# First attention of a two-block network: scores from stacked fp32r halves, tiles in another order, modulation spread over later stages

## The chip, the cores and the metric

The kernel runs on one core of a Trainium2 chip. The metric is the device time of one execution in microseconds (us), the median of several runs.

## The reference

One sequence of 512 tokens, 1024 wide, passes through three mixers and a lookup of experts. All is float32.

```python
def first_block(x, c, ...):
    for i in range(2):
        h, gate = adaln_norm(x, c, norm_g[i], ada_w[i], ada_b[i])
        y = nsa_mixer(h, ...) if i == 0 else dilated_mixer(h, ...)
        x = x + gate * y
    return rms_norm(x, final_g)
# adaln_norm: shift, scale, gate = split(silu(c) @ w_ada + b_ada, 3)
#             h = rms_norm(x, g) * (1 + scale) + shift
# nsa_mixer: compressed, selected and window attention, 16 query heads, 2 key heads of 64
#            (at 512 tokens the selected and the window branch see every earlier token)
# dilated_mixer: 16 heads, three dilation patterns, groups joined by their softmax sums
def second_block(x, c, ...):
    mod = silu(c) @ ada_w + ada_b            # six parts of 1024
    # sliding-window attention and a short convolution, then:
    h2 = modulate(rmsnorm(x, norm2_g), shift2, scale2)
    x = x + gate2 * peer(h2, ...)            # 8 heads x 16 of 16384 experts per token
```

The three modulation products, `silu(c) @ ada_w`, have 96 blocks of 128 outputs in all: twelve chunks of eight blocks, each chunk the sum of eight weight pieces.

## The kernel before

Weights come as one stream of pieces of 128 x 1024 floats (`stream()`, line 73) into a ring of four buffers, loaded by SyncE in stream order (`ask_pieces`, L211). A buffer is free again when its piece was split (most pieces) or used (raw ones). A split piece becomes two fp32r tiles, its rounded upper half by ScalarE (`split_hi`, L232) and the rest by GpSimd (`split_lo`, L240); a projection is then three fp32r products per 128 x 128 block (L264, L276). Three split pieces can be held, and the list of pieces is fixed, so a stage's engines work in a written order; stages are blocks with a barrier of all engines between them.

The modulation pieces ("ada") are raw. VectorE multiplies each by its column of silu(c) and adds it to a running row sum (`ada_piece`, L322 and L325); TensorE then reduces a chunk over the partitions with 16 one-column f32 instructions (`ada_chunk`, L333). Chunks 0 to 2 belong to the first two stages, the other nine (3 to 11) lie in the first attention as its fillers.

**Stage 2** (L801 on) makes the first mixer's projections, rotates queries and keys into `qr` (ten rows: two of keys, eight of query pairs), does the compressed branch, and ends with the eight `z` units. GpSimd's last work there is the split of the last `z` piece; ScalarE ends it with the last evacuation (L913).

**First attention** (`attention("nsa", ...)`, L1062 to L1275). A unit is one head of one query tile of 128 tokens in one branch (selected or window): 2 branches x 4 tiles x 16 heads = 128 units, in that order, tile i with i+1 key blocks. Two heads share 128 partitions (64 rows each), so the keys are copied first into `ks_pad`, where the other head's rows are zero (L1160, L1179 and the memsets L1206, L1207); the first product waits for these. Of unit n, in the written order of TensorE:

```python
pe.matmul(ps[:, n % SB, 0:len(vb) * P], q, k, start=True, stop=True)   # L1132, f32, 128 x (i+1)*128
# transposes of unit n-3 (L1140), fillers, products with v of unit n-5 (L1152)
```

VectorE takes the masked minimum of the negated scores (L1189), every fourth copy of transposed probabilities (L1112), the modulation filler (`ada_dve`: 0, 0.5, 0.75 or 1 piece per unit with 1, 2, 3, 4 key blocks), and at the end of every eight units the gated result (L1238). ScalarE takes the exponentials with their sum (L1169) and the other copies (L1110), GpSimd the additions into the result (L1248). Scores have three buffers, so TensorE is at most three units ahead.

Later stages: output projection with modulation of `mod[:, 24:96]`, dilated projections (32 units) and attention, output projection, the second block's projections (18 units), window attention, output projection, and the query projection of the lookup (16 units and 16 score groups).

**Last stage** (L2080 on). 128 tiles of the table `u`, then 128 of `v`, each 128 x 1024 floats. SyncE loads tile m into one of three `t_raw` buffers when tile m-3 is lowered; ScalarE makes the upper half (`upper`, L2194), GpSimd the lower (`lower`, L2268), TensorE multiplies: 24 products of 384 columns per `u` tile (L2124), 18 of 512 per `v` tile (`down`, L2160). In the second half, per four tiles, VectorE also weighs (L2430) and lowers (L2436) the weights and adds four gathered rows (L2447), and GpSimd issues four indirect loads of rows (L2289).

Of the kernel before, what the change touches and what calls it, by code (L numbers as in the profile page):

```python
# [28 lines left out]
P = 128  # L29
# [42 lines left out]

def stream():
# [17 lines left out]
    load("ada", 72)  # L91
    load("nsa_out", 8)
    for name, count in (("dq", 8), ("dk", 8), ("dv", 8), ("dz", 8), ("dil_out", 8), ("q2", 4), ("k2", 1), ("v2", 1), ("cc", 4), ("cu", 4), ("cb", 4), ("out2", 8),
                        ("wq", 16), ("subkeys", 2)):
        load(name, count)
# [13 lines left out]
def build(nc, w_stream, consts_in, small_dram, x_in, pos_in, perm_in, u_in, v_in, u_rows, out, gates_dram, gelu_dram):  # L109
    ctx = ExitStack()  # L110
    with ctx:
# [200 lines left out]
        def ada_piece(dve, j, sums):  # L312
# [5 lines left out]
            total = sums[:, chunk % 2, :]  # L318
# [9 lines left out]
        def ada_chunk(pe, chunk, sums, bank):  # L328

            pe.wait_ge(ada_used, (chunk + 1) * KD)  # L330
            for b in range(KD):
                col = chunk * KD + b
                mm = pe.matmul(ps[:, bank, col:col + 1], sums[:, chunk % 2, b * P:(b + 1) * P],  # L333
                               C("ones")[:, 0:1], start=True, stop=True)
# [465 lines left out]

        with phase() as block:  # L801
# [100 lines left out]
            def _(act):  # L902
# [40 lines left out]
                for u in range(15, 23):  # L943
# [9 lines left out]
                    elif u == 20:  # L953
                        cmp_copy(3)
                        for r in Z_RAW:
# [4 lines left out]
            def _(pool):  # L960
# [4 lines left out]
                for u, n in enumerate(parted, 2):  # L965
# [3 lines left out]
                    if 5 <= u < 12:  # L969
                        rope_nsa[1](pool, u - 5)  # L970

# [90 lines left out]
        def attention(tag, block, units, work, finish, finish_pool=None, pe_filler=None, dve_filler=None, ask=0,  # L1062
                      pads=(), pad_units=1, prob_at=WR_AT,
                      act_filler=None, pool_filler=None, pe_first=None, act_first=None, dve_first=None, sink_neg=None):
# [54 lines left out]
            def _(pe):  # L1119
                if pe_first:  # L1120
                    pe_first(pe)
                for n in range(N + LP):
                    if n < N:
# [8 lines left out]
                        pe.matmul(ps[:, n % SB, 0:len(vb) * P], q, k, start=True, stop=True).then_inc(s_done.sem, 1)  # L1132
# [83 lines left out]
        ks_pad = place("ks_pad", WR_AT + 4 * T, [2, 2, T])  # L1216
        nsa_units = []
        for branch, (ku, vt) in enumerate(((0, vs), (1, vw))):
            for i in range(TT):
                for h in range(NH):  # L1220
                    g = h // 8
                    nsa_units.append((qr[:, 2 + h % 8, tile_tokens(i)], ks_pad[:, g, ku, 0:(i + 1) * P],
                                      C("causal")[:, T - (i + 1) * P:T],
                                      [vt[:, b, g * DH:(g + 1) * DH] for b in range(i + 1)], BIG))
# [4 lines left out]
        def nsa_finish(dve, g, o, den, nmax, o_read):  # L1229
            branch, i, half = g // 8, (g // 2) % 4, g % 2  # L1230
# [10 lines left out]
        def nsa_finish_pool(pool, o_read):  # L1241
            for g in range(16):
                i, half = (g // 2) % 4, g % 2
                o_read.wait(pool, g + 1)
                if g >= 8:
                    pool.wait_ge(added, g - 7)
                dst = ot[:, i, half * 512:(half + 1) * 512]
                pool.tensor_tensor(dst, dst, gtmp[:, g % 2, :], ALU.add).then_inc(added, 1)  # L1248

# [1411 lines left out]
```

## Time and profile before

| | us |
|---|---|
| median of 3 runs | 2348.06 |
| lowest, highest | 2342.16, 2350.55 |
| the profiled execution | 2357.37 |
| its span, first to last instruction | 2355.6 |
| TensorE busy in it | 2238.0 |
| VectorE, ScalarE, GpSimd busy | 1530.1, 914.9, 1307.7 |
| first attention, from its first to its last instruction | 219.7 to 446.9 |
| tiles of `v`, first to last product | 1805.7 to 2346.1 |

Positions are microseconds from the start of the profiled span. The span holds all instructions; the profiled execution's own time is 1.8 us longer and 9.3 us above the median of the runs, which had no profile. "Granted clock" is the share of full speed at which TensorE was clocked, 1.00 for 2.4 GHz and 0.50 for 1.2 GHz. In the groups of instructions, `x` is their number, followed by their busy time and the mean duration of one; an f32 product appears as two instructions, an fp32r product as one.

### The profile page before, as it was taken

Reading aid. Unit: us, or ns where it says so; the run is one execution under the profiler, and the core shown is the slowest. Engines: PE = TensorE matmul, PEld = TensorE weight load, DVE = VectorE, ACT = ScalarE, POOL = GpSimd, SP = SyncE. Lnnn points to the kernel's source line nnn. Section 1 sums busy time; section 2 is a strip of 40 time slices with the busy share of each in tenths; the row PEclk is TensorE's granted clock in tenths of the full one; section 3 lists DMA queues with packets and bytes.
Section 4 is the critical chain, followed back from the end, with each engine's and each line's share of the span. In section 5 each row is a group of like instructions: output and inputs, shape, how many; then the busy total and the mean of one; then the engine's idle time right before and its main releaser. Section 6 shows DMA issues by size and latency. Waiting matters only on the chain.

```text
span 2355.6 us, 31939 instructions
## 1 busy us (share of the span) xinstructions
PE 2238.0 (95%) x11801; PEld 1963.8 (83%) x11801; DVE 1530.1 (65%) x2977; ACT 914.9 (39%) x1513; POOL 1307.7 (56%) x691
## 2 busy tenths in 40 slices
PE   4999999889989989889999999999999999999999
PEld 4888787778878878777899999999999778787877
DVE  6625878556215534542399999999993766676656
ACT  2224555332236332532234333455553333333332
POOL 0532010137540234123268888766656999999996
PEclk9999999789999989999999999999999999999999
DMA  7243646323210122022258888899988999999996
GB/s 266 90 138 104 204 157 211 100 75 107 91 62 5 68 72 81 10 81 94 68 176 293 281 278 279 302 362 355 327 329 324 334 347 336 343 343 347 336 340 246
DMA packets 164474, 492.39 MB, mean 209 GB/s; under 512 B 15072, under 2 KB 64608, under 8 KB 162912
## 3 DMA queue, kind: packets, MB, share of 16 engines
q1 hardware_dynamic: 107872, 305.79, 38.1%
q0 software_dynamic: 36864, 134.23, 15.7%
q10 hardware_dynamic: 19584, 50.34, 5.6%
q8 instruction: 94, 1.54, 0.3%
q14 instruction: 60, 0.49, 0.1%
HBM read 437.87 MB, written 52.43 MB: 208 GB/s over the span
## 4 chain that ended last, share of the span: by engine, by line
POOL 19%; PE 16%; DVE 12%; DMA 2%; issue 1%; ACT 0%; DVEq 0%; ACTq 0%; POOLq 0%
POOL t_split L2268 12%; PE ps L2124 10%; POOL arena L2289 7%; PE ps L2142 4%; PE ps L2160 2%; DMA t_raw<-v_table 2%; DVE arena L2355 1%; DVE arena L2346 1%; DVE arena L2347 1%; DVE arena L2386 1%; DVE arena L2351 1%; DVE arena L2342 1%; DVE rope L2324 1%; DVE arena L2381 1%; DVE norm_rows L2324 1%
## 5 line engine op out<-in xcount | busy, mean ns | idle before, releaser
L2268 POOL TENSOR_TENSOR t_split<-t_raw,t_split 128x1024 fp32r<-128x1024 f32 x256 | 628.1, 2454 | 145.2 <-ACT t_split L2194 141.8
L240 POOL TENSOR_TENSOR w_split<-ring,w_split 128x1024 fp32r<-128x1024 f32 x113 | 272.5, 2415 | 510.7 <-ACT w_split L232 499.4
L2124 PE MATMUL ps<-h_hi,t_split 128*128 128x384 f32 x2048 | 537.1, 338 | 5.7 <-ACT e_gel L2200 3.0
L2160 PE MATMUL ps<-t_split,w_split 128*128 128x512 f32 x2304 | 532.6, 391 | 9.7 <-POOL t_split L2268 7.8
L2160 PEld LDWEIGHTS ps<-t_split,w_split 128*128 128x128 f32 x2304 | 429.3, 188 | 112.9 <-POOL t_split L2268 19.6
L264 PE MATMUL ps<-h_hi,w_split 128*128 128x512 f32 x1440 | 451.7, 392 | 0.0
L2194 ACT ACTIVATE t_split<-t_raw 128x1024 fp32r<-128x1024 f32 x256 | 270.3, 1057 | 360.3 <-DMA t_raw<-v_table 230.0
L2124 PEld LDWEIGHTS ps<-h_hi,t_split 128*128 128x128 f32 x2048 | 373.3, 189 | 8.1 <-POOL t_split L2268 4.6
L2124 PE MATMUL ps<-h_lo,t_split 128*128 128x384 f32 x1024 | 343.6, 336 | 0.0
L264 PEld LDWEIGHTS ps<-h_hi,w_split 128*128 128x128 f32 x1440 | 270.4, 188 | 56.5 <-issue 0.7
L264 PE MATMUL ps<-h_lo,w_split 128*128 128x512 f32 x720 | 280.2, 389 | 0.0
L232 ACT ACTIVATE w_split<-ring 128x1024 fp32r<-128x1024 f32 x113 | 119.0, 1057 | 360.0 <-PE ps L264 220.9
L2430 DVE TENSOR_TENSOR arena<-arena 128x1536 f32<-128x1536 f32 x32 | 108.5, 3389 | 168.5 <-DMA arena<-gates_scratch 168.4
L2289 POOL DMA_INDIRECT arena<-v_table,arena x128 | 193.6, 1512 | 20.7 <-issue 20.0
L2124 PEld LDWEIGHTS ps<-h_lo,t_split 128*128 128x128 f32 x1024 | 193.7, 189 | 0.0
L2200 ACT ACTIVATE e_gel<-ps 128x384 f32<-128x384 f32 x128 | 63.0, 492 | 326.6 <-PE ps L2124 294.6
L2447 DVE SCALAR_TENSOR_TENSOR ps<-arena,ps 128x1024 f32<-128x1024 f32 x127 | 163.0, 1283 | 15.1 <-DMA arena<-v_table,arena 8.6
L264 PEld LDWEIGHTS ps<-h_lo,w_split 128*128 128x128 f32 x720 | 135.2, 188 | 28.4 <-issue 0.7
L1152 PE MATMUL ps<-arena 128*128 128x64 f32 x916 | 138.0, 280 | 0.0
L1248 POOL TENSOR_TENSOR arena<-arena,gtmp 128x512 f32<-128x512 f32 x16 | 20.3, 1271 | 205.7 <-DVE gtmp L1238 205.7
L1152 PEld LDWEIGHTS ps<-arena 128*128 128x128 f32 x916 | 132.4, 209 | 2.1
L2421 DVE TENSOR_SCALAR arena<-ps,arena 128x128 f32<-128x128 f32 x384 | 130.5, 401 | 0.0
(317 smaller groups left out, 3199.3 us busy)
## 6 DMA issues: line engine op xcount, KB each, us to landing
ring<-w_stream SPq DMA_DIRECT2D x219, 512.0 KB, 3.4
t_raw<-u_table SPq DMA_DIRECT2D x128, 512.0 KB, 4.6
t_raw<-v_table SPq DMA_DIRECT2D x128, 512.0 KB, 4.9
gelu_scratch<-e_gel ACTq DMA_DIRECT2D x128, 192.0 KB, 4.8
gates_scratch<-arena ACTq DMA_DIRECT2D x8, 3072.0 KB, 12.7
arena<-gelu_scratch SPq DMA_DIRECT2D x32, 768.0 KB, 5.4
arena<-gates_scratch SPq DMA_DIRECT2D x32, 768.0 KB, 8.8
xT<-x_in SPq DMA_DIRECT2D x2, 1024.0 KB, 10.8
```

The source lines that it names most:

```text
L232: act.activation(w_split[:, i % RS, 0, :], ring[:, n % R, :], ACT.Copy).then_inc(hi_done, 1)
L240: pool.tensor_tensor(w_split[:, i % RS, 1, :], ring[:, n % R, :], w_split[:, i % RS, 0, :].bitcast(F32), ALU.subtract).then_inc(lo_done, 1)
L264: mm = pe.matmul(ps[:, bank, :], w[:, a, k * P:(k + 1) * P], src[b][:, k, :], start=(k + a + b == 0), stop=(k == KD - 1 and a == 1))
L1152: mm = pe.matmul(ps[:, 5 + (m // 8) % 2, (m % 8) * DH:(m % 8 + 1) * DH], prt[:, m % TB, b * P:(b + 1) * P], v, start=(b == 0), stop=(b == ...
L2124: mm = pe.matmul(ps[:, 6 + n % 2, 0:NT], t_split[:, n % RAWS, u, k * P:(k + 1) * P], h_parts[h][:, k, P:T], start=(k + u + h == 0), stop=( ...
L2160: mm = pe.matmul(ps[:, 2 * i + half, :], w_split[:, b % 2, w, at:at + P], t_split[:, m % RAWS, v, half * 512:(half + 1) * 512], start=(n + ...
L2194: act.activation(t_split[:, m % RAWS, 0, :], t_raw[:, m % RAWS, :], ACT.Copy).then_inc(t_hi, 1)
L2268: pool.tensor_tensor(t_split[:, m % RAWS, 1, :], t_raw[:, m % RAWS, :], t_split[:, m % RAWS, 0, :].bitcast(F32), ALU.subtract).then_inc(t_ ...
L2289: pool.indirect_dma_start(out=vrows[j % NBV][:, :], out_offset=None, in_=v_in, in_offset=bass.IndirectOffsetOnAxis(ap=idx[:, j:j + 1], axis=0)
L2421: dve.tensor_scalar(hot_a[:, r * QT + s, :], ps[:, 3, 0:P], selT[:, 0, t + s:t + s + 1], selT[:, 2, t + s:t + s + 1], ALU.is_equal, ALU.mu ...
L2430: dve.tensor_tensor(gel, gel, gateb[:, s, :].rearrange("p (c e t) -> p e c t", e=VB, t=CHUNK), ALU.mult).then_inc(weighed, 1)
L2447: dve.scalar_tensor_tensor(out=acc, in0=vrows[j % NBV], scalar=w_tok[:, j:j + 1], in1=acc, op0=ALU.mult, op1=ALU.add).then_inc(v_added, 1)
```

## The change

Five edits.

1. **Scores.** Queries are split into an upper fp32r half and a rest, stacked on the 128 partitions of one operand (`q_first`, `q_second`, `q_lower`); the keys' upper half stands twice under one another (part 0 of `k_stack`), and so does their rest (part 1). A score tile is then two fp32r products, (upper + rest of q) with each part. `ks_pad`, its memsets and copies are gone.
2. **Preparing.** The eight key pieces and the first query tile are made at the end of stage 2: five ScalarE activations and five GpSimd subtractions of 64 x 1024, the latter after its last split. Seven more query tiles are made during the attention (`turn_upper` at the start and at units 1, 4, 18, 48, 56, 64; `turn_lower` on GpSimd among its additions), and TensorE waits for them at the start of their groups of eight.
3. **Order.** Units run by half (of the heads), branch, tile; the tiles in the order 2, 0, 3, 1, and in the last group of four 2, 0, 1, 3. The additions on GpSimd each wait for the one before.
4. **Modulation.** Five chunks (3 to 7) stay in the attention, at 40/310 of a piece per key block and unit; chunk 8 goes to the end of the dilated projections, 9 and 10 into the second block's projections (after units 12 and 17), 11 into the lookup's query projection. Their pieces lie between the weight pieces of the same stages, in the same ring.
5. **Last stage.** Of each four `v` tiles but the first four, the second is lowered by VectorE (`table_lower`, after the four row additions), not by GpSimd: 31 tiles.

```diff
+ADA6, ADA9, ADA12 = range(27, 31), (4, 5, 6, 7, 12, 13, 14, 15), (7, 8, 9, 10)
...
-    load("ada", 72)
+    load("ada", 40)
     load("nsa_out", 8)
+    with_modulation(["dq"] * 8 + ["dk"] * 8 + ["dv"] * 8 + ["dz"] * 8, ADA6)
+    load("dil_out", 8)
+    with_modulation(["q2"] * 4 + ["k2", "v2"] + ["cc"] * 4 + ["cu"] * 4 + ["cb"] * 4, ADA9)
+    load("out2", 8)
+    with_modulation(["wq"] * 16, ADA12)
...
+        k_stack = place("k_stack", 0, [2, 2, 2, T], F32R)
+        q_first = place("q_first", 4096, [8, P], F32R)
+        def key_upper(act, g, half):
+            act.activation(k_stack[rows_of(half), 0, g], qr[rows_of(g), 0:2, :], ACT.Copy).then_inc(stack_hi, 1)
+        def key_lower(pool, g, half):
+            pool.tensor_tensor(k_stack[rows_of(half), 1, g], qr[rows_of(g), 0:2, :],
+                               k_stack[rows_of(g), 0, g].bitcast(F32), ALU.subtract).then_inc(stack_lo, 1)
...
+                pool.wait_ge(lo_done, split_of[piece_of(22)] + 1)
+                pool.wait_ge(stack_hi, 2)
+                key_lower(pool, 0, 0)
+                pool.wait_ge(stack_lo, 1)
+                key_lower(pool, 0, 1)
...
-                        pe.matmul(ps[:, n % SB, 0:len(vb) * P], q, k, start=True, stop=True).then_inc(s_done.sem, 1)
+                        if pe_ready:
+                            pe_ready(pe, n)
+                        for j, part in enumerate(k):
+                            mm = pe.matmul(ps[:, n % SB, 0:len(vb) * P], q, part, start=(j == 0), stop=(j == len(k) - 1))
+                        mm.then_inc(s_done.sem, 1)
...
-        NSA_ADA = 9 * KD
-        ada_pace, ada_after, due = (0, 0, 0.5, 0.75, 1.0), [], 0.0
+        NSA_ADA = 5 * KD
+        ada_pace, ada_after, due = [40 * b / 310 for b in range(5)], [], 1e-6
...
+                rope_dil[3].wait(pe, 16)
+                ada_chunk(pe, 8, ada_sum6, 4)
...
+                    if u in (12, 17):
+                        rope_two[4].wait(pe, 5)
+                        ada_chunk(pe, 9 + u // 17, ada_sum9, 5)
...
+                n2.dve_gain(dve)
+                for j in range(8):
+                    ada_piece(dve, 9 * KD + j, ada_sum9)
                 dve.wait_ge(q_sum, 1)
...
+                for u in range(4):
+                    for j in range(2 * u, 2 * u + 2):
+                        ada_piece(dve, 10 * KD + j, ada_sum9)
...
+                    for j in {5: range(0, 4), 7: range(4, 8)}.get(u, ()):
+                        ada_piece(dve, 11 * KD + j, ada_sum12)
...
+        def on_dve(m):
+            return m >= PK + VB and (m - PK) % VB == 1
...
+                def table_lower(m):
+                    dve.wait_ge(t_hi, m + 1)
+                    dve.tensor_tensor(t_split[:, m % RAWS, 1, :], t_raw[:, m % RAWS, :],
+                                      t_split[:, m % RAWS, 0, :].bitcast(F32), ALU.subtract).then_inc(t_lo_dve, 1)
...
                     v_add(4 * b + 2)
                     v_add(4 * b + 3)
+                    if b + 1 < NVB:
+                        table_lower(PK + VB * (b + 1) + 1)
```

## Rows read from the trace of the kernel before

**Rows 1.** The page, part 1: busy time of TensorE, its share of the span.

```profile
PE 2238.0 (95%) x11801; PEld 1963.8 (83%) x11801; DVE 1530.1 (65%) x2977; ACT 914.9 (39%) x1513; POOL 1307.7 (56%) x691
```

**Rows 2.** Busy times by stretch: whole attention, 50 us of it; each engine, clock, DMA.

```profile
219.70:446.90 227.20, 218.47 (x1360) 177.98 (x1360) 171.64 (x409) 114.79 (x354) 21.44 (x18) 0.90 0.51 167
378.00:428.00 50.00, 49.99 (x305) 38.41 (x303) 42.90 (x79) 24.16 (x60) 3.82 (x3) 0.93 0.66 216
```

**Rows 3.** Groups of instructions, forms apart, 222 to 430 us.

```profile
L325 DVE SCALAR_TENSOR_TENSOR ada_sum<-ring,csil,ada_sum 128x1024 f32<-128x1024 f32 x63 | 82.1, 1302 | 0.0
...
L1132 PE MATMUL ps<-ks_pad,arena 128*128 128x512 f32 x64 | 37.0, 660 | 0.0
L1132 PE MATMUL ps<-ks_pad,arena 128*128 128x384 f32 x64 | 30.3, 558 | 0.0
...
L1132 PE MATMUL ps<-ks_pad,arena 128*128 128x256 f32 x64 | 21.8, 424 | 0.0
...
L333 PE MATMUL ps<-cst,ada_sum 128*128 128x1 f32 x128 | 15.0, 247 | 0.0
...
L1169 ACT ACTIVATE prob_nsa<-arena 128x128 f32<-128x128 f32 x32 | 12.8, 399 | 7.4 <-DVE arena L1189 7.2
```

**Rows 4.** Timeline: score products of neighbouring units, one key block, then four.

```profile
228.72 0.44 PE L1132 MATMUL ps<-ks_pad,arena 128*128 128x128 f32 x2
...
229.28 0.44 PE L1132 MATMUL ps<-ks_pad,arena 128*128 128x128 f32 x2
...
424.37 1.08 PE L1132 MATMUL ps<-ks_pad,arena 128*128 128x512 f32 x2
...
426.56 0.65 PE L1132 MATMUL ps<-ks_pad,arena 128*128 128x512 f32 x1
```

**Rows 5.** Last chain, in order of time: runs of fp32r products of 384, 512 columns.

```profile
1741.20 4.16 PE ps L2124 x24
...
2313.17 33.37 PE ps L2160 x144
```

**Rows 6.** Busy times by stretch: a modulation chunk, and the stretch behind it.

```profile
349.90:353.30 3.40, 3.40 (x29) 3.30 (x29) 1.73 (x8) 1.63 (x6) 0.00 (x0) 1.00 0.67 200
353.30:356.70 3.40, 3.40 (x14) 2.83 (x14) 2.11 (x6) 1.47 (x5) 0.00 (x0) 0.50 0.29 114
```

**Rows 7.** Timeline at the attention's start and at its last chunk.

```profile
219.70 0.95 POOL L1206 MEMSET ks_pad<- 64x1024 f32 x1 [14.30 <-POOLq L801]
...
222.13 1.37 PE L1132 MATMUL ps<-ks_pad,arena 128*128 128x128 f32 x8 [3.34 <-POOL ks_pad L1207]
...
430.54 2.42 PE L333 MATMUL ps<-cst,ada_sum 128*128 128x1 f32 x16 [2.46 <-DVE ada_sum L325]
```

**Rows 8.** Timeline of VectorE in the second block's projections.

```profile
879.57 0.20 DVE L1738 TENSOR_SCALAR arena<-ps 128x40 f32<-128x40 f32 x1 [24.99 <-PE ps L1671]
```

**Rows 9.** Groups of instructions, forms apart, tiles of v, 1810 to 2330 us.

```profile
L2268 POOL TENSOR_TENSOR t_split<-t_raw,t_split 128x1024 fp32r<-128x1024 f32 x122 | 298.2, 2444 | 10.9 <-ACT t_split L2194 8.7
L2289 POOL DMA_INDIRECT arena<-v_table,arena x127 | 192.6, 1517 | 20.6 <-issue 19.9
...
L2430 DVE TENSOR_TENSOR arena<-arena 128x1536 f32<-128x1536 f32 x30 | 102.9, 3429 | 142.4 <-DMA arena<-gates_scratch 142.4
L2436 DVE TENSOR_TENSOR w_split<-arena,w_split 128x1536 fp32r<-128x1536 f32 x31 | 82.4, 2658 | 20.1 <-ACT w_split L2227 20.1
```

**Rows 10.** Line L2160: durations ns, first and last start.

```profile
L2160 PE MATMUL ps<-t_split,w_split x2304: 387/389/504, 1805.7 to 2346.1; 128*128 128x512 f32 x192
```

**Rows 11.** Waits, 1806 to 2346 us: total, times, longest.

```profile
PEld ps L2160 <- POOL t_split L2268: 19.6, 31, 1.7
...
PE ps L2160 <- POOL t_split L2268: 7.8, 20, 1.2
```

**Rows 12.** Timeline of VectorE: beside a GpSimd subtraction, and without one.

```profile
2000.23 4.30 DVE L2436 TENSOR_TENSOR w_split<-arena,w_split 128x1536 fp32r<-128x1536 f32 x1 [1.54 <-ACT w_split L2227]
...
2016.07 1.79 DVE L2436 TENSOR_TENSOR w_split<-arena,w_split 128x1536 fp32r<-128x1536 f32 x1 [0.51 <-ACT w_split L2227]
```

More of the change, by code:

```diff
@@ L1212, in attention @@
             return nmax, den
[L1216 to L1224 removed]
+        q_lower = place("q_lower", HR_AT + 8 * T, [8, T], F32R)
@@ new lines, in build, with queries @@
+        q_second = place("q_second", HR_AT + 2 * T, [8, P], F32R)
+        groups = [(half, branch, i) for half in range(2) for branch in range(2)
+                  for i in (ORDER_LAST if half and branch else (FIRST,) + NEXT)]
+        turns = [(0, i) for i in NEXT] + [(1, i) for i in (FIRST,) + NEXT]
+        def queries(half, i):
+            if half == 0:
+                return q_first if i == FIRST else q_lower[:, :, tile_tokens(i)]
+            at = ((FIRST,) + NEXT).index(i)
+            return (q_second, q_first, q_lower[:, :, tile_tokens(NEXT[0])], q_lower[:, :, tile_tokens(NEXT[1])])[at]
@@ new lines, in build, with turn_upper @@
+        nsa_units = []
+        for half, branch, i in groups:
+            for h in range(8):
+                nsa_units.append((queries(half, i)[:, h, :], [k_stack[:, part, half, branch, 0:(i + 1) * P] for part in range(2)],
+                                  C("causal")[:, T - (i + 1) * P:T],
+                                  [(vs, vw)[branch][:, b, half * DH:(half + 1) * DH] for b in range(i + 1)], BIG))
+        def turn_upper(act, t):
+            half, i = turns[t]
+            act.activation(queries(half, i)[rows_of(half)], qr[rows_of(half), 2:10, tile_tokens(i)],
+                           ACT.Copy).then_inc(turn_hi, 1)
@@ L1225, in build, with nsa_act_filler, nsa_pe_ready @@
+        def nsa_act_filler(act, n, o_read):
+            if n in TURN_AT:
+                if n >= 48:
+                    o_read.wait(act, n // 8 - 1)
+                turn_upper(act, TURN_AT[n])
+        def nsa_pe_ready(pe, n):
+            half, branch, i = groups[n // 8]
+            if n % 8 == 0 and branch == 0 and (half, i) in turns:
+                pe.wait_ge(turn_lo, turns.index((half, i)) + 1)
         gr = area(WORK + 3840, 2, 8)
@@ L1264, in ada_pe @@
         def ada_pe(pe, n):
-            for chunk in range(9):
+            for chunk in range(5):
                 last = (chunk + 1) * KD - 1
@@ L2075, in tile_us, with lowered @@
             return 4.17 * n + 2.3 * min(max(n - GATE_AT, 0), QUADS // 2)
+        t_lo_dve = sem("t_lo_dve")
+        def on_dve(m):
+            return m >= PK + VB and (m - PK) % VB == 1
+        def lowered(eng, m):
+            if on_dve(m):
+                eng.wait_ge(t_lo_dve, (m - PK) // VB)
+            else:
+                eng.wait_ge(t_lo, sum(not on_dve(i) for i in range(m + 1)))
         def table_tile(m):
```

154 lines of the change are left out of this document (109 added, 45 removed).

## The prediction

> **What bounds the kernel now.** The page comes first: TensorE is busy 95% of the span [rows 1]. Such a share hides stages with other limits, so I then read busy times by stretch. In the first attention TensorE is busy 218 of 227 us at a mean granted clock of 0.90, and in its heaviest 50 us it never rests, with VectorE at 43 of 50 and ScalarE at 24 [rows 2]. The timeline gives the pitch: with four key blocks one unit starts 2.19 us after the other, with one block 0.56 us [rows 4]. The stage is TensorE's own work at four blocks and nearly so at two and three; at one block the exponential's 0.40 us [rows 3] and the copy behind it fill most of the pitch on ScalarE, so there TensorE isn't alone. Among the tiles of v TensorE is busy too, but 2304 products take 540.4 us [rows 10], 4.22 us a tile, where an undisturbed run of eight tiles takes 33.37 [rows 5], 4.17 a tile. The waits name GpSimd's subtraction as what the weight loads wait for, 19.6 us in 31 waits, and the products 7.8 us [rows 11].
>
> **The change, part by part.** The sum is made against the profiled execution, 2357.37 us; that is 9.3 us above the median of the runs, and I take the differences over to the median.
>
> *Scores.* An f32 product is two instructions. Both together show 1.08 us at 512 columns, one alone 0.65 [rows 4], so the second starts 0.43 us behind the first and the pair holds TensorE 0.86 us, 0.215 per key block. An fp32r product of 384 columns costs 4.16 / 24 = 0.173 us, one of 512 costs 33.37 / 144 = 0.232 [rows 5]; the line through both gives 0.114 at 256. The new pair is thus 0.464, 0.347, 0.228 us against 0.86, 0.645, 0.43: saved 0.396, 0.298, 0.202 us in each of 32 units of four, three and two blocks, 28.7 us. For one block I take nothing, because ScalarE sets that pitch. No fp32r product of 128 columns is in the trace: its price lies between 0.06 us (the same line) and 0.215 us (each of the two as dear as the whole f32 pair), so those 32 units lie between a gain of 3 us and a loss of 7. I take zero, nearest to the ScalarE row. Bounds for the wide ones: 24 us (0.25 us a product, some wait in it) to 33 us (0.43 saved at 512 and in proportion).
>
> *Modulation.* A chunk is 16 instructions [rows 3], 1.9 us with its loads. Four leave the attention, -7.5 us, and come back where dense projections keep TensorE full: +7.6 us, and 0.3 us for VectorE's read of the sum ahead of the barrier after the dilated projections. The VectorE pieces move too, 32 x 1.30 = 42 us of its 172 [rows 2, 3]. Where they land VectorE has room: it idles 25.0 us in the second block's projections before q's variances [rows 8], and eight pieces there are 10.4 us. They wait for the ring, since a piece is only asked for when the one four before it is split; by the order written the eighth lands some 5 us before that variance is due. In the dilated projections the pieces stand behind the last transposed v, when VectorE has nothing else to do, and in the lookup's projection they hold the evacuation of units 5 and 7 by about 4 us, where TensorE needs the bank three units (16 us) later. If that cover were gone, each late piece would cost at least its 1.3 us. So zero.
>
> *Clock.* The stretch with a chunk has TensorE busy 3.40 of 3.40 us at 1.00, and the next 3.4 us are granted 0.50, 1.2 GHz [rows 6]. I found this behind seven of the eight chunks before the last. Each costs about half of 3.4, 1.7 us. Four chunks fewer: 3.5 x 1.7 = -6 us. In the dense stages no chunk is in the trace behind full projections except the one before the attention, and no drop was seen there during it, so nothing is added back. Bounds: 0 and -10.
> The Trainium skill (TensorE: Matmul & The Clock Gate, HAM oscillation) puts such drops down to gaps in which TensorE is idle. By that rule moving chunks would give nothing on the clock, since they leave no gap; the trace shows the drop without any gap, and I go by the trace. By the rule the sum would be 6 us smaller.
>
> *Start and end of the attention.* GpSimd's memsets hold the first product until 222.13, 3.34 us [rows 7]. They go; the first exponential still waits for its table and now for one query activation of about 1.05 us ahead of it. I take -1.5 us. The last chunk waited 2.46 us for VectorE [rows 7]; at half the pieces per unit that goes, -2.5 us. What is late next is the drain of five heavy units, unchanged in both orders.
>
> *What preparing costs.* GpSimd idles 14.3 us before the barrier [rows 7]; five subtractions of 64 x 1024, at the 2.44 us of a 128-row one [rows 9], are 12.2 us, and their four waits on semaphores 0.2 each: it fits by about 1 us. I take +0.5; if it doesn't fit, the overrun is paid in full. The five activations on ScalarE stand ahead of evacuations which have 3 us of room. Inside the attention seven activations (7 us) and seven subtractions (17 us) are added. TensorE waits for them only at eight group starts, each made at least eight units ahead. But the subtractions meet VectorE's two-input instructions: one of those that takes 1.8 us alone took 4.30 beside a subtraction [rows 12]. Seven such meetings at up to 2.4 us, half of them under cover, with ScalarE's in narrow groups: +5 us (0 to 15). Each changed tile also meets buffers of the other width; that is in the 5.
>
> *Last stage.* Per four tiles GpSimd has 4 x 2.44 + 4 x 1.52 = 15.8 us [rows 9] of a pitch of 16.9. With one subtraction less it has 13.4, and is no longer last. TensorE's waits for it are 7.8 to 19.6 us in all [rows 11]; part of them began with a late load of `t_raw`, which stays. I take -9 us, between 540.4 - 128 x 4.17 = 6.6 and 19.6. VectorE has 3.43 + 2.66 + 4 x 1.28 = 11.2 us per four tiles and gets 1.2 (1024 columns by the 1.8 us for 1536) to 3.6 more, while it waits 142.4 / 31 = 4.6 us per four tiles for gate loads [rows 9]. The new wait is on ScalarE's upper half; behind it stand the next weighing and two row additions, needed by TensorE more than two tiles (8 us) later. So it hides.
>
> Sum: -28.7 + 0.4 - 6 - 1.5 - 2.5 + 0.5 + 5 - 9 = -41.8 us, 2315.6 for the profiled execution, 2306 against the median. A measurement of this kernel can tell about 0.3%, 7 us, from no change.
>
> **Rivals.**
> - *The attention becomes VectorE's and ScalarE's.* After the change VectorE has 172 - 42 = 130 us of some 185, more than 70%, and every unit passes score, minimum, exponential, transposes in turn. If handshakes set the pace at one and two blocks, and clock drops come with them, half of the scores' and all of the clock's gain is lost: -42 + 14 + 6 = -22, 2326. Against it: VectorE kept up at 43 of 50 us with TensorE never idle [rows 2].
> - *The scores were hidden anyway,* the change's main part doing nothing: -13, 2335. Against it stands the pitch, which is TensorE's busy time.
> - *Everything goes well:* the last stage gets all 19.6 us, the narrow products 3 and the drain runs at full clock, half of 15 us: -62, 2286.
> - *Slower: VectorE becomes the chain of the v tiles.* Its gate waits don't shrink, because it can't reach them behind the wait for the upper half, and the added subtraction takes 3.6 us beside GpSimd. Then four tiles take 11.2 + 3.6 + 4.6 + 0.6 = 20.0 us instead of 16.9: 31 x 3.1 = +96, less the rest's -33: 2411. It decides from 1.1 us per four tiles on (33 / 31). The Trainium skill (GPSIMD Engine Reference, section 2) has the two engines share an SBUF interface that two-input VectorE instructions need, which is what would feed this. Against it: the gate loads are issued by SyncE, which doesn't wait for the added instruction, so they land in the meantime; and the shared time per four tiles falls, 2.44 us of GpSimd against 1.2 of VectorE.
>
> **How the numbers follow.** Forecast (2296 to 2320) 0.60, VectorE and ScalarE 0.15, hidden 0.06, all well 0.13, slower 0.04; another 0.02 for no change. The range leaves out the two last and the ends of the others: 2288 to 2329. Faster 0.93, same 0.03, slower 0.04.
>
> **What would show it.** In the changed profile: score products half as long per unit and a pitch of about 1.8 us at four blocks; the attention from about 219.8 to 408; fewer stretches at 0.50 inside it; the first product right behind the barrier; GpSimd's last subtraction of stage 2 within a microsecond of ScalarE's last evacuation; four chunks of 1.9 us in later stages without a wait before them; tiles of v in about 531 us, with GpSimd's waits gone from TensorE's list. Wrong would be: TensorE waiting for exponentials in wide units; the stage before ending late on GpSimd; VectorE's lowered tile among the releasers of L2160; a pitch at one block above 0.7 us.

## The result, and the profile after

The changed kernel took 2312.94 us, the median of five runs (2309.76 to 2323.31); the kernel before 2348.06 in runs beside them (2342.16 to 2355.64). The ratio is 0.9857, with a 95% interval from 0.9825 to 0.989: faster, by 35 us. Forecast were 2306 us and a range from 2288 to 2329. The profiled execution was the longest of the five, 2323.31 us with a span of 2321.2, 34.1 us under the one before.

The page, part 1, answers to [rows 1]: TensorE is busy 33 us less, VectorE 29 us more, GpSimd 60 us less.

```profile
PE 2204.6 (95%) x11801; PEld 1970.8 (85%) x11801; DVE 1558.9 (67%) x3010; ACT 924.5 (40%) x1524; POOL 1247.5 (54%) x670
```

Busy times by stretch answer to [rows 2]: the whole attention, then 50 us of it (length, PE, PEld, DVE, ACT, POOL with their counts, the granted clock, DMA).

```profile
222.50:424.70 202.20, 183.34 (x1296) 170.36 (x1296) 142.97 (x376) 119.46 (x360) 36.52 (x23) 0.88 0.32 105
...
277.00:327.00 50.00, 45.97 (x310) 42.81 (x308) 34.32 (x92) 29.10 (x86) 10.22 (x7) 0.83 0.31 98
```

The attention is 25 us shorter, but TensorE now stands still for 19 of its 202 us, where it was 9 of 227, and its mean granted clock is 0.88 instead of 0.90. The score products show the price that was forecast. In the timeline of the last heavy tile units start 1.35 us apart while the lighter ones ahead still drain, then 1.79, which answers to the 2.19 us of [rows 4].

```profile
406.78 0.71 PE L1190 MATMUL ps<-k_stack,q_lower 128*128 128x512 f32 x2
408.13 0.70 PE L1190 MATMUL ps<-k_stack,q_lower 128*128 128x512 f32 x2
409.92 0.48 PE L1190 MATMUL ps<-k_stack,q_lower 128*128 128x512 f32 x1
```

What TensorE waits for inside the attention (total, times, longest) is new: the copies behind the transposes, which come from the exponential before them.

```profile
PE ps L1199 <- ACT arena L1165: 12.8, 13, 2.0
PE ps L346 <- DVE ada_sum L338: 1.7, 2, 1.0
```

The timeline around the longest of these pauses shows where it begins, VectorE first, then ScalarE, then TensorE. A modulation piece of 2.19 us stands ahead of a narrow unit's minimum; the exponential waits 2.02 us for that minimum, the next copy for the exponential, and TensorE 1.98 us for the copy. The piece ran beside an addition on GpSimd; the next one, alone, took 1.27 us.

```profile
240.43 2.19 DVE L338 SCALAR_TENSOR_TENSOR ada_sum<-ring,csil,ada_sum 128x1024 f32<-128x1024 f32 x1
242.54 0.28 DVE L1248 CUSTOM_DVE_ANT_0 arena<-ps,cst 128x128 f32<-128x128 f32 x1
...
242.86 0.40 ACT L1228 ACTIVATE prob_nsa<-arena 128x128 f32<-128x128 f32 x1 [2.02 <-DVE arena L1248]
243.26 0.26 ACT L1165 ACTIVATE arena<-ps 128x128 f32<-128x128 f32 x1
...
243.66 0.30 PE L1199 MATMUL ps<-cst,prob_nsa 128*128 128x128 f32 x1 [1.98 <-ACT arena L1165]
```

At the start of the attention, answering to [rows 7], GpSimd is through with the prepared keys at 220.5 us, ScalarE with its last evacuation at 222.2, and the first product comes 0.94 us behind the stage before instead of 3.34. Two pauses of TensorE follow within 7 us, of 1.25 and 1.62, which the kernel before doesn't have.

```profile
215.68 4.86 POOL L826 TENSOR_TENSOR k_stack<-arena,k_stack 64x1024 fp32r<-64x1024 f32 x2
...
221.61 0.60 ACT L941 ACTIVATE arena<-ps 128x512 f32<-128x512 f32 x1 [6.71 <-PE ps L277]
...
222.52 1.69 PE L1190 MATMUL ps<-k_stack,q_first 128*128 128x384 f32 x7 [0.94 <-PEq L829]
```

In the tiles of `v`, answering to [rows 9 to 11], the first group is the products' first and last start, the second all that TensorE waited for in the stage, the third the groups of instructions from 1792 to 2300 us.

```profile
L2304 PE MATMUL ps<-t_split,w_split x2304: 387/389/504, 1789.1 to 2311.8; 128*128 128x512 f32 x192
...
PE ps L2304 <- DVE w_split L2581: 1.5, 1, 1.5
PE ps L2304 <- issue: 0.2, 1, 0.2
...
L2412 POOL TENSOR_TENSOR t_split<-t_raw,t_split 128x1024 fp32r<-128x1024 f32 x93 | 224.6, 2415 | 74.4 <-ACT t_split L2338 73.3
L2433 POOL DMA_INDIRECT arena<-v_table,arena x128 | 184.1, 1438 | 24.8 <-issue 18.1
...
L2575 DVE TENSOR_TENSOR arena<-arena 128x1536 f32<-128x1536 f32 x31 | 58.5, 1889 | 9.6 <-DMA arena<-gates_scratch 9.5
```

TensorE's waits for GpSimd, 7.8 and 19.6 us before, are gone, and the stage takes 522.7 us instead of 540.4. The chain that ended last has one piece of 506.29 us for 2232 products, 4.08 us a tile, and this, not 4.17, is TensorE's own pitch.

```profile
1805.91 506.29 PE ps L2304 x2232
```

### The profile page after: what moved, and what is told of

Its sections match the earlier page's. It is cut to its first block, busy times and chain, and to the rows that moved or that the text cites. A ratio compares the mean times of both kernels' runs of the same rounds, so it can differ in the third digit from the quotient of the medians.

```text
span 2321.2 us, 31989 instructions
## 1 busy us (share of the span) xinstructions
PE 2204.6 (95%) x11801; PEld 1970.8 (85%) x11801; DVE 1558.9 (67%) x3010; ACT 924.5 (40%) x1524; POOL 1247.5 (54%) x670
## 4 chain that ended last, share of the span: by engine, by line
PE 36%; DVE 12%; POOL 1%; DMA 1%; issue 0%; ACT 0%; DVEq 0%; ACTq 0%
PE ps L2304 23%; PE ps L2268 10%; PE ps L2286 4%; DVE arena L2500 1%; DVE arena L2491 1%; DVE arena L2492 1%; DVE arena L2531 1%; DVE arena L2496 1%; DVE arena L2487 1%; DVE rope L2469 1%; DVE arena L2526 1%; DVE norm_rows L2469 1%; DVE arena L2469 1%; DVE arena L2534 1%; POOL t_split L2412 1%; DVE arena L2507 0%
## 5 line engine op out<-in xcount | busy, mean ns | idle before, releaser
L2412 POOL TENSOR_TENSOR t_split<-t_raw,t_split 128x1024 fp32r<-128x1024 f32 x225 | 549.5, 2443 | 210.5 <-ACT t_split L2338 207.6
L2304 PE MATMUL ps<-t_split,w_split 128*128 128x512 f32 x2304 | 522.9, 389 | 1.6 <-DVE w_split L2581 1.5
L2433 POOL DMA_INDIRECT arena<-v_table,arena x128 | 184.1, 1438 | 24.8 <-issue 18.1
L2581 DVE TENSOR_TENSOR w_split<-arena,w_split 128x1536 fp32r<-128x1536 f32 x32 | 92.7, 2895 | 107.5 <-ACT w_split L2371 107.5
L1248 DVE CUSTOM_DVE_ANT_0 arena<-ps,cst 128x128 f32<-128x128 f32 (+3 forms) x192 | 81.7, 433 | 83.3 <-PE ps L1190 82.0
```

Of the source, the lines that this page charges most:

```text
L2304: mm = pe.matmul(ps[:, 2 * i + half, :], w_split[:, b % 2, w, at:at + P], t_split[:, m % RAWS, v, half * 512:(half + 1) * 512], start=(n + ...
L2412: pool.tensor_tensor(t_split[:, m % RAWS, 1, :], t_raw[:, m % RAWS, :], t_split[:, m % RAWS, 0, :].bitcast(F32), ALU.subtract).then_inc(t_ ...
L2433: pool.indirect_dma_start(out=vrows[j % NBV][:, :], out_offset=None, in_=v_in, in_offset=bass.IndirectOffsetOnAxis(ap=idx[:, j:j + 1], axis=0)
```

## The experiments

Twelve kernels ran, each against the kernel before on the same chip, in three groups and a last one. Ratios compare across groups; microseconds only within one.

**The changed kernel again** (no edit).

> The changed kernel once more, on the chip of the next three runs. Expected 2313 us (2309 to 2317): its five runs beside the record gave 2309.8 to 2323.3.

Measured: 2313.85 us (2311.46 to 2315.89), ratio 0.9851 (0.983 to 0.9871).

**The last stage as before.**

```diff
         def on_dve(m):
-            return m >= PK + VB and (m - PK) % VB == 1
+            return False
...
-                    if b + 1 < NVB:
-                        table_lower(PK + VB * (b + 1) + 1)
```

> The changed kernel with the last stage as before: GpSimd subtracts for all 128 tiles. Theory: GpSimd was last there in nearly every tile, and TensorE's own pitch is the 4.08 us that it shows in the changed kernel, so that the whole difference of 540.8 to 523.1 us between the two profiles belongs to this edit: 2313 + 17 = 2330 (2326 to 2333), and the late loads of t_raw come back with it. Rival, as predicted: TensorE's own pitch is 4.17 us, the edit is worth 9 and the rest of the 17.7 us came from a less disturbed run: 2322 (2319 to 2325).

Measured: 2329.87 us, ratio 0.9936 (0.9913 to 0.9959), 16.0 us above the changed kernel on the same chip. The edit is worth what the profiles' difference said, about twice the forecast. With the edit taken back the tiles of `v` take 539.5 us again (1777.9 to 2317.4), and the other changes of the stage go with it: ScalarE waits 226.7 us for `t_raw`, VectorE 149.8 us for gates, and its weighing takes 3512 ns.

**Nine chunks in the attention again.**

```diff
-    load("ada", 40)
+    load("ada", 72)
...
-        NSA_ADA = 5 * KD
-        ada_pace, ada_after, due = [40 * b / 310 for b in range(5)], [], 1e-6
+        NSA_ADA = 9 * KD
+        ada_pace, ada_after, due = [72 * b / 310 for b in range(5)], [], 1e-6
```

> The changed kernel with all nine modulation chunks in the first attention again, its 72 pieces spread evenly over the key blocks as the 40 are now. Theory: a chunk brings a stretch at half clock with it, in the attention alone. Four chunks more are 7.5 us of instructions and, with one stretch of 3.4 us each, 6.8 us of clock; the later stages give back 5: 2313 + 7.5 + 6.8 - 5 = 2322. If each brings two or three stretches, as four of the five do now, 15 instead of 6.8: 2330. Rival: the clock drops anyway in the attention, chunks only decide where: 2313 + 7.5 - 5 = 2315.5, with as many microseconds at 0.50 inside the attention as now (48).

Measured: 2347.9 us, ratio 0.9993 (0.9979 to 1.0008), 34 us above the changed kernel. All three numbers (2315.5, 2322, 2330) missed by far, and this run turned the study round: four chunks, for which the forecast paid 5.6 us, are worth 34 beside the new scores. It isn't quite the old arrangement of the nine chunks: the kernel before laid no pieces into the tiles of one key block, and here they are spread evenly. Its attention, in one row, has TensorE idle for 26 of 240 us with VectorE busy 182, and a granted clock of 0.80; the two rows behind it are one pause of 1.39 us, with VectorE busy throughout, and the 17.1 us at half clock that came after it. A chunk's products stand there too, from 289.5 us on.

```profile
220.00:459.80 239.80, 213.33 (x1360) 198.10 (x1360) 182.29 (x408) 121.13 (x360) 36.60 (x22) 0.80 0.49 159
...
287.00:289.20 2.20, 0.81 (x8) 0.69 (x8) 2.20 (x7) 1.10 (x4) 0.00 (x0) 0.99 0.48 127
289.20:306.30 17.10, 17.10 (x80) 16.50 (x79) 7.01 (x24) 6.36 (x26) 1.27 (x1) 0.50 0.28 88
```

**A chunk's eight products spread over eight units.**

```diff
-                if n == min(next(i for i, a in enumerate(ada_after) if a > last) + 2, len(nsa_units) - 1):
+                start = min(next(i for i, a in enumerate(ada_after) if a > last) + 2, len(nsa_units) - 1)
+                if start < len(nsa_units) - 1 and start <= n < start + KD:
+                    ada_column(pe, 3 + chunk, n - start)
```

> The changed kernel with the eight one-column products of each modulation chunk in the attention issued one per unit, over eight units, instead of all eight behind one unit (the last of the five stays as it is). The same instructions in all. Theory: it is the run of sixteen short instructions and their weight loads that brings the clock down behind a chunk; 30.7 us at 0.50 stand behind the first four now, which cost half of that. If they go: 2313 - 15 = 2298 (2295 to 2302), with 17 us at 0.50 left inside the attention. Rival: the attention's own mixture of short instructions, transposes and pauses brings the clock down and the chunk is only the place: no more than 3 us from 2313, and 40 to 50 us at 0.50 inside.

Measured: 2307.68 us (2300.5 to 2322.68), ratio 0.9831 (0.9802 to 0.9861). Its interval overlaps that of the changed kernel, and its profile has 48.7 us at 0.50 in the attention, 30.7 of them in one piece from 295 us on, far from any run of short products; three pauses of 0.74 to 1.10 us stand in the 7 us ahead of it. So a run of short products isn't needed for the half clock. That spreading them gains nothing isn't shown: the profiled execution took 2319.64 us, 12 above the median, and three of the six took 2300.5 to 2304.07 us, at mean granted clocks of 0.975 to 0.978 instead of its 0.968.

**The modulation part alone** (f32 scores, last stage as before; five chunks in the attention).

> The kernel before with the modulation part of the change alone: four of the nine chunks leave the first attention, the rest keeps the old pace in proportion; scores and the last stage as before. Prediction's terms: +0.4 and the clock's -6, so 2343 (2338 to 2347). Theory now: the chunks were cheap beside f32 scores, because VectorE had time for its pieces there, and became dear only when the scores got short; the same 2343. Rival: moving them is worth the same with either kind of scores, 34 us as between the changed kernel with nine chunks (2347.9) and with five (2313.9): 2315.

Measured: 2338.68 us, ratio 0.9956 (0.9939 to 0.9973), 10 us under the kernel before. So the forecast's 5.6 us, or 8 with the last chunk's wait, were about right for this part by itself, and the 34 us belong to its meeting with the new scores.

**Nine chunks, light pieces.**

```diff
+            wide = PIECE if j < 3 * KD or k == 0 else P
+            total = total[:, 0:wide]
...
-                dve.scalar_tensor_tensor(out=total, in0=ring[:, piece % R, :], scalar=c, in1=total,
+                dve.scalar_tensor_tensor(out=total, in0=ring[:, piece % R, 0:wide], scalar=c, in1=total,
```

> The changed kernel with all nine chunks in the attention (2347.9), where seven of eight VectorE pieces of a chunk work on 128 of their 1024 columns only; this leaves most of those modulation sums out. TensorE's work is untouched. VectorE theory: it is VectorE's pieces, 72 x 1.5 us in a stage that would otherwise take 190 us, that make TensorE pause at the score buffers, and the clock falls behind the pauses. Then nearly all comes back but the chunks' own instructions: 2313.9 + 7.5 - 5 = 2316 to 2322. Chunk theory: the runs of sixteen one-column instructions bring the clock down (85 us at 0.50 inside the attention against 41): it stays at 2340 or more.

Measured: 2302.07 us, ratio 0.9823 (0.9792 to 0.9854), 40 us under the same kernel with whole pieces (0.9993 - 0.9823 = 0.017). With all nine chunks' products still on TensorE the half clock shrank from 95.6 to 17.1 us.

**Nine chunks, whole pieces, hardly any products.**

```diff
+            if chunk >= 3:
+                mm = pe.matmul(ps[:, bank, chunk * KD:(chunk + 1) * KD], sums[:, chunk % 2, 0:P],
+                               C("ones")[:, 0:KD], start=True, stop=True)
```

> The changed kernel with all nine chunks in the attention (2347.9), VectorE's pieces in full, but TensorE's eight one-column products of a chunk replaced by one product of eight columns; this leaves most of the modulation out. Fourteen instructions fewer per chunk, 9 x 1.7 = 15 us of TensorE. Chunk theory: those instructions also bring most of the 85 us at 0.50; they go: 2348 - 15 - 30 = 2303. VectorE theory: VectorE's 72 pieces set the time, so TensorE's saved work is mostly waited away and the half clock stays: 2335 to 2345, with 60 us or more at 0.50.

Measured: 2332.62 us, ratio 0.9914 (0.9894 to 0.9934), with 78.5 us at 0.50. Of the 30 us of clock that the chunk theory promised 8.6 came, half of 95.6 less 78.5. The two rows, light pieces first, tell it apart: VectorE 124 or 181 us busy, TensorE idle 10 or 27, clock 0.95 or 0.82.

```profile
220.60:406.30 185.70, 175.41 (x1360) 163.65 (x1360) 123.92 (x408) 120.44 (x360) 35.78 (x22) 0.95 0.61 205
```

```profile
220.90:441.00 220.10, 192.68 (x1234) 176.74 (x1234) 181.05 (x408) 120.98 (x360) 36.51 (x22) 0.82 0.53 173
```

**No pieces in the narrow tiles.**

```diff
-        ada_pace, ada_after, due = [40 * b / 310 for b in range(5)], [], 1e-6
+        ada_pace, ada_after, due = [0, 0] + [40 * b / 287 for b in range(2, 5)], [], 1e-6
```

> The changed kernel with no VectorE pieces in the tiles of one key block; the 40 pieces are spread over the tiles of two to four blocks in proportion to their blocks, as before in kind. Theory: two half-clock stretches of the attention (behind 244.8 and 285.7 us) follow pauses in which a piece stands ahead of a narrow unit's minimum; they cost 7 to 8 us and go: 2306 to 2309. Rival: the pieces only meet the wide units more closely and the pauses come elsewhere: 2312 to 2316.

Measured: 2313.86 us, ratio 0.9847 (0.9828 to 0.9865): no difference. The pause at 240 went and others came in the wide tiles; TensorE still rests 17 us.

**Everything but the scores' part.**

> The kernel before with the modulation part and the last stage's part of the change, without the scores' part (f32 scores, light tiles first, nothing prepared in the stage ahead). Prediction's terms: the scores and what belongs to them are worth 28.7 + 1.5 + 2.5 - 5 - 0.5 = 27 us, so this should be 2314 + 27 = 2341, 0.9966 of before. Theory now, from the ratios of the parts run so far (0.9956 for the modulation alone, 0.9851 / 0.9936 for the last stage): 0.987 of before, 2318, and the scores' part is worth 5 us at most, because VectorE's pieces now make TensorE pause 17 us in the attention and 24 us more of it run at half clock.

Measured: 2321.49 us (2321.04 to 2325.84), ratio 0.9884 (0.9867 to 0.99). The scores' part, for which the forecast had 27 us, adds 0.3% of the whole, 7 to 8 us, and the edges of the two intervals touch. The attention in its profile and in that of the changed kernel's second run:

```profile
222.60:426.20 203.60, 199.46 (x1296) 163.26 (x1296) 135.21 (x376) 111.90 (x352) 19.10 (x15) 0.94 0.31 104
```

```profile
219.50:421.60 202.10, 183.53 (x1296) 171.32 (x1296) 141.78 (x376) 119.50 (x360) 36.07 (x22) 0.87 0.32 105
```

**The changed kernel with light pieces.** The edit of the nine chunks' light pieces, for the attention's five.

> The changed kernel, where seven of eight VectorE pieces of the attention's five chunks work on 128 of 1024 columns; this leaves most of those modulation sums out. TensorE's work is untouched. Theory: those pieces cost 10 us of TensorE's pauses and, behind these, 25 us at 0.50 instead of 1.00, 12 us: 2314 - 22 = 2292, 0.976 of before, with about 20 us at 0.50 left in the attention. Rival: the pauses come from the handshakes of score, minimum, exponential and transposes at the changes from wide to narrow tiles, which stay: 2308 or more, 0.983.

Measured: 2294.27 us (2289.91 to 2297.48), ratio 0.9759 (0.9741 to 0.9776), as the theory said, with 21.4 us at 0.50 in the attention. VectorE is busy 32 us less than in the row above, and the stage 23 us shorter with TensorE's work the same. TensorE still rests 10.0 of its 179 us, so the pieces aren't all of it: in one pause, 1.10 us at 285.4, the activation that makes a query tile (1.06 us) stood ahead of the exponential on ScalarE, and no whole piece ran:

```profile
220.90:399.80 178.90, 168.94 (x1296) 158.15 (x1296) 109.47 (x376) 119.89 (x360) 35.71 (x22) 0.94 0.36 119
```

**Half pieces.**

```diff
-                ada_piece(dve, 3 * KD + j, ada_sum)
+                ada_half(dve, 3 * KD + j // 2, j % 2)
```

> The changed kernel with each VectorE piece of the attention's chunks cut in two of 512 columns, 80 instead of 40, each half behind a unit of its own. The same arithmetic, VectorE's work some 2 us longer in all. Theory: a whole piece holds a unit's minimum for 1.5 us, longer than the three units of lead in the narrow tiles; a half holds it 0.8 us, so pauses of over half a microsecond go from 13 to 5 or fewer and some of the half clock with them: 2300 to 2306, 0.980. Rival: it is VectorE's sum of work that limits, not the length of one piece: 2312 to 2316.

Measured: 2318.08 us, ratio 0.987 (0.9852 to 0.9889). The theory got no support: no gain, 14 pauses of over half a microsecond instead of 13, if shorter ones (1.46 us at most instead of 1.98). But the run doesn't tell the length of a piece from VectorE's sum of work. A half took 931 ns in the mean, far more than half of a piece, so the sum grew too, 65.1 us of these instructions instead of 52.7:

```profile
L1379 DVE SCALAR_TENSOR_TENSOR ada_sum<-ring,csil,ada_sum 128x512 f32<-128x512 f32 x70 | 65.1, 931 | 0.0
```

**Three chunks in the attention, three in the dilated projections.**

```diff
-ADA6, ADA9, ADA12 = range(27, 31), (4, 5, 6, 7, 12, 13, 14, 15), (7, 8, 9, 10)
+ADA6, ADA9, ADA12 = range(19, 31), (4, 5, 6, 7, 12, 13, 14, 15), (7, 8, 9, 10)
...
-        ada_pace, ada_after, due = [40 * b / 310 for b in range(5)], [], 1e-6
+        ada_pace, ada_after, due = [0, 0, 0] + [24 * b / 215 for b in range(3, 5)], [], 1e-6
...
+                    for j in {12: (0, 1), 13: (2, 3)}.get(r, ()):
+                        ada_piece(dve, 6 * KD + j, ada_sum6)
```

> The changed kernel with two more of the five chunks moved out of the attention, into the dilated projections behind VectorE's rotations (three chunks there, three in the attention); the attention's 24 pieces stand only in tiles of three and four key blocks, where three units leave VectorE 1.7 to 2.6 us of room for a piece of 1.5, and a chunk's eight products are issued one per unit. Theory (VectorE's work in the attention is what is left to win): 16 pieces of 1.5 us fewer there, half of what the light pieces took away, give 10 us or more; moved instructions cost the dilated projections 4 us; the rest of the pauses over half a microsecond falls to 6 or fewer and half clock in the attention below 30 us: 2314 - 10 - 4 + 4 - 4 = 2300 (2294 to 2306), 0.979 of before. Rival: the moved pieces hold the rotations or the turned v in the dilated projections as VectorE's pieces there take 2.5 us beside GpSimd's subtraction, or the clock goes its own way: 2308 or more.

A chunk's products are also issued one per unit here, as in the run above that spreads them.

Measured: 2304.38 us (2301.42 to 2314.12), ratio 0.9828 (0.9801 to 0.9855). The lowest median of the versions that compute everything, clearly below the kernel before; against the changed kernel (0.9851) the intervals overlap, so "faster than that" isn't shown. The profile says both where the theory held and where it was undone. The attention fell from 202.1 to 169.8 us with the clock at 0.99; but the tiles of `u` begin only 14.7 us earlier (1134.1 against 1148.8). Of the 32 us half went again behind it, the largest part in the dilated projections: first row the attention, then TensorE's two pauses there, then VectorE's pieces, which stood waiting for their loads and took 2 to 3 us each.

```profile
220.60:390.40 169.80, 158.46 (x1264) 147.14 (x1264) 119.02 (x360) 119.38 (x360) 36.67 (x22) 0.99 0.23 76
...
551.56 0.47 PE L277 MATMUL ps<-h_hi,w_split 128*128 128x512 f32 x1 [2.31 <-ACT arena L1555]
566.32 0.77 PE L277 MATMUL ps<-h_hi,w_split 128*128 128x512 f32 x1 [8.63 <-issue]
...
545.31 3.22 DVE L338 SCALAR_TENSOR_TENSOR arena<-ring,csil,arena 128x1024 f32<-128x1024 f32 x1 [2.75 <-DMA ring<-w_stream]
559.83 2.07 DVE L338 SCALAR_TENSOR_TENSOR arena<-ring,csil,arena 128x1024 f32<-128x1024 f32 x1 [7.58 <-DMA ring<-w_stream]
```

## Why the prediction was right, and where it was wrong

That the number was right is in good part luck, because errors stood against each other: the scores' part gave some 19 us less than forecast, the last stage 7 to 11 more and the modulation 4 more. By the ratios the whole 1.5% is 0.4% of modulation (0.9956), then 0.7% of the last stage (0.9884), then 0.3% of scores (0.9851).

| part of the change | forecast, us | measured, us |
|---|---|---|
| scores, their order and preparation | -27 | -8 |
| modulation, its clock, without the last chunk's wait | -5.6 | -10 |
| last stage | -9 | -16 to -20 |

**Scores.** The price of the products was right. Length times mean granted clock is what the attention would take at full clock: 203.6 x 0.94 = 191.4 us without the scores' part, 202.1 x 0.87 = 175.8 with it. TensorE's idle time in these rows rose from 4.1 to 18.6 us. So the work itself fell by 15.6 + 14.5 = 30 us, against 28.7 forecast. The step that failed is "new work in the attention, +5", and with it the dismissal of the first rival: the pauses cost 14.5 us. And time at half clock, 0.06 and 0.13 of the two lengths lost, cost 14 us more. Together they ate the gain; the attention is 1.5 us shorter, and its start, 3.1 us earlier, makes most of the rest of the 5.3 us between the two spans. One of the prediction's own signs of being wrong appeared, TensorE waiting on ScalarE in wide units, as here with four key blocks, and one of its signs of being right came in number only: there were seven stretches at 0.50 instead of nine, but 47.8 us of them instead of 45.8.

```profile
355.27 0.63 PE L1199 MATMUL ps<-cst,prob_nsa 128*128 128x128 f32 x4 [1.10 <-ACT arena L1165]
```

The argument against that rival was that VectorE kept up at 43 of 50 us while TensorE never rested [rows 2]. It did so with an f32 pitch of 2.19 us; a shorter pitch takes away the room, not the work. The forecast even wrote down 130 us of some 185 for VectorE; measured were 142 of 202. A share of 70% looks harmless, but the units pass four engines in turn with three units of lead. By an estimate, a piece of 1.5 us is more than the room which three units of two blocks leave: 3 x (0.91 - 0.60) = 0.9 us, where 0.91 is the pitch measured at 320.53 us and 0.60 VectorE's minimum (0.42), its reading (0.08) and a quarter of a copy (0.42). No run shows that this length is what counts: halves of 0.93 us gained nothing, and with their larger sum they couldn't decide it. What is shown is the price of the pieces: 32 us of VectorE's work less made the stage 23 us shorter, 8.6 of it in TensorE's idle time (18.6 to 10.0) and some 15 in clock (51.3 to 21.4 us at 0.50). How much light pieces would give beside f32 scores wasn't run.

**Modulation.** By itself the move gave what was expected, some 10 us. What wasn't foreseen is that its worth depends on the scores: 10 us beside f32 products, 34 beside fp32r ones. Turned round, the new scores with nine evenly spread chunks would make the kernel slower: the ratio 0.9993 holds the last stage's 0.7 to 0.85%, so without it 1.0065 to 1.0078, 15 to 18 us above the kernel before. That kernel wasn't run; the figure is worked out. The moved chunks took 1.84 us each in their new places, and the two in the second block's projections and the last had a clock of 1.00 around them:

```profile
904.09 1.84 PE L346 MATMUL ps<-cst,arena 128*128 128x1 f32 x16
903.00:908.00 5.00, 5.00 (x32) 4.40 (x31) 3.35 (x4) 1.06 (x1) 2.37 (x1) 1.00 0.91 285
```

**Clock.** Forecast: half a stretch of 3.4 us per chunk, four fewer, -6 us. With f32 scores that reading held, five chunks with a stretch of half clock behind each, as here, where TensorE had been busy 3.20 of 3.20 us:

```profile
265.20:268.40 3.20, 3.20 (x28) 3.01 (x27) 1.70 (x4) 1.03 (x3) 0.00 (x0) 1.00 0.48 161
268.40:271.80 3.40, 3.40 (x13) 2.64 (x12) 0.57 (x2) 1.08 (x3) 0.00 (x0) 0.50 0.36 136
```

With the new scores the place held and the size didn't. In the first profile a stretch begins within 2 us of each of the five chunks' ends, but these five are 34.0 us, 6.8 each and not 3.4; two more, 13.6 us, begin 1.1 and 1.4 us behind pauses of 1.98 and 1.32. Neither a chunk nor a pause is enough by itself: nine chunks with light pieces had only 17.1 us at 0.50, behind four of the nine, and nine with whole pieces and hardly a product 78.5, and the pause of 1.39 us at 287 us, behind which 17.1 us at half clock stood in the kernel with nine whole chunks, stands in the one without their products too, at full clock until 301.5. What the runs do show is that light pieces take most of the half clock away: 51.3 to 21.4 us with five chunks, 95.6 to 17.1 with nine.

The Trainium skill (TensorE: Matmul & The Clock Gate, HAM oscillation) puts the half clock down to idle gaps of TensorE. The prediction set that rule aside on the strength of the rows before. For the changed kernel the rule points the right way, since more pauses came with more half clock, while the row at 268.4 shows that it isn't the whole. How long a half-clock stretch lasts once it has begun, 3.4 us or 30.7, the traces leave open, and runs of one kernel differ with it: of the twelve with nine whole chunks the shortest, 2339.8 us, had a mean granted clock of 0.965 and the longest, 2352.9, one of 0.958.

**Start, preparing, last chunk.** Preparing fitted with 1.7 us to spare (220.5 against 222.2), so its +0.5 didn't fall due. The first product came 2.4 us sooner behind the barrier, against 1.5 forecast, but the two new pauses behind it, 1.25 and 1.62 us, take this back: the start gave nothing. In the first profile its being early doesn't show in its position (222.52 after 222.13), because the stage before ran at half clock for 17.1 us around 140 us instead of 6.8, ahead of anything that the change touches; in the second run of the kernel it stands at 219.48. The last chunk's wait, 2.46 us before, is gone in the changed kernel, as forecast.

**Last stage.** Here the mechanism was right and the size off. The floor was read from one run of eight tiles at the very end, 33.37 us [rows 5]; over 124 tiles without a wait it is 4.08, so 540.4 - 128 x 4.08 = 18 us were to be had, and all came. The prediction also kept back what "began with a late load of `t_raw`". Those late loads followed from GpSimd: SyncE asks for a tile only when the tile in its buffer is lowered; ScalarE's waits for `t_raw` fell from 230.0 to 54.3 us with the edit and were 226.7 without it. Two further guesses fell well: the 142.4 us for which VectorE waited for gates were slack and shrank to 9.5, and its weighing got faster, 1889 ns instead of 3429, because it no longer met GpSimd: in the kernel before 24 of 30 weighings ran beside a subtraction for more than 0.2 us, in the changed kernel one of 30 did, and those without any took 1758 and 1752 ns. So the slower rival stayed far off; the added subtraction took 1.33 us.

## What to carry to other kernels

When the bounding engine's work is made shorter, price what the others do in the new pitch before booking the gain: their work per unit against the new time per unit, and the longest other instruction on their queue against the room that the units of lead leave. Here the first looked harmless at 70%, the second was never worked out, and the runs show that the pieces cost the gain, not which of the two sets the cost. Two edits of which one fills an engine and the other shortens the cover can't be priced one by one; run the pair and each alone. And take an engine's own pitch from the longest run without a wait that the trace has, not from a run that merely looks undisturbed.

## What the runs showed of the hardware that was not expected

- An fp32r product of 128 columns has no surcharge: a narrow unit's pitch with two of them is 0.53 us (238.31 to 238.84), where two instructions of an f32 product gave 0.56, and TensorE's next instruction starts 0.25 us behind the first of the pair (238.31 to 238.56) instead of 0.28 (228.72 to 229.00).
- VectorE's piece of 1024 columns takes 1325 ns in the mean with GpSimd busy 19 us in the attention, 1506 with 36 us, and 2023 in the dilated projections of the last kernel beside GpSimd's subtractions, for the same work. In the changed kernel's second profile 22 of 35 pieces met nothing on GpSimd and took 1278 ns, the nine that overlapped it for more than 0.5 us took 2140. The Trainium skill (GPSIMD Engine Reference, section 1) has both engines share SBUF interfaces, with contention for instructions of two SBUF inputs such as these; the traces agree and give the size.

```profile
L338 DVE SCALAR_TENSOR_TENSOR ada_sum<-ring,csil,ada_sum 128x1024 f32<-128x1024 f32 x35 | 46.4, 1325 | 0.0
```

```profile
L338 DVE SCALAR_TENSOR_TENSOR arena<-ring,csil,arena 128x1024 f32<-128x1024 f32 x21 | 42.5, 2023 | 27.9 <-DMA ring<-w_stream 27.1
```

- Stretches at 1.2 GHz of very different length, 3.4 to 30.7 us, begin close behind pauses of TensorE of only 0.7 to 2 us. Behind one of 1.39 us, with a chunk's products next to it, stood 17.1 us, 8.6 us lost; the same pause without the products had no half clock behind it. Which of the two a stretch needs isn't settled.
